# Where rows begin in SBUF: h buffers with rows 832 columns apart instead of 772, the context at column 544, and everything behind them moved by 32 bytes

## The reference

```python
for l in range(DEPTH):                                   # DEPTH = 2
    sh1, sc1, gt1, sh2, sc2, gt2 = split(silu(c) @ w_ada[l] + b_ada[l])      # and the same of c_ctx
    h  = rmsnorm(x,   g_mix[l]) * (1 + sc1)  + sh1       # latent tokens
    hc = rmsnorm(ctx, g_mix[l]) * (1 + csc1) + csh1      # context tokens
    q, k, v, u = split_in(h @ w_in[l])                   # hc goes through the same weights
    a_out  = latent_attention(rope(q), rope(k), v, k_ctx, v_ctx, attn_sink[l])
    cv_out = silu(layernorm(depthwise_conv31(glu(u))))
    x = x + gt1 * (concat(rmsnorm(a_out), rmsnorm(cv_out)) @ w_out[l])
    h2 = rmsnorm(x, g_ffn[l]) * (1 + sc2) + sh2
    x = x + gt2 * ((silu(h2 @ w_gate) * (h2 @ w_up)) @ w_down[l])             # D_FF = 2816
    # the context goes the same way in layer 0; in layer 1 only its keys and values are needed
return rmsnorm(x, g_final)
```

## The kernel before

| operand of a gemm | start before | length of a row | start after | length of a row after |
|---|---|---|---|---|
| weights, `w_high`, `w_low` | 0 | 512, so all 0 | 0 | the same |
| `h_high`, `h_low`, columns from 0 | 0, 16, 32 ... 112 for k = 0 to 7 | 3,088 | 32 for every k | 3,328 |
| the same, context | 8, 24 ... 120 | | 32 for every k | |
| `ff_high`, `ff_low`, both ranges | 32 for every k | 3,072 | 32 | 3,072 |
| `attn_high`, `attn_low`, both ranges | 0 for every k | 3,072 | 32 | 3,072 |
| `conv_high` / `conv_low` | 0 and 64 in turn / 0 | 3,264 / 3,072 | 32 and 96 / 32 | the same |
| `k_stacked`, `q_stacked`, `prob`, `v_tokens`, `probT` | 0 | multiples of 128 | 32 | the same |
| `ff_last_*`, `h_normal_*` | 0 | 2,048 | 0 | 2,048 |

## Time and profile before

### The profile page before, as it was taken

The page is one execution under the profiler, slowest core; times in us unless marked ns, Lnnn a source line. Parts: engine busy times, 40 slices in busy tenths (PEclk is TensorE's granted clock), DMA queues, the critical chain, the costliest instruction groups (busy, mean ns, idle before and its releaser), DMA issues.

```text
span 1577.4 us, 22649 instructions
## 1 busy us (share of the span) xinstructions
PE 1519.3 (96%) x8802; PEld 1229.0 (78%) x8802; DVE 919.2 (58%) x1511; ACT 537.1 (34%) x866; POOL 128.6 (8%) x163
## 2 busy tenths in 40 slices
PE   6999988999999999999999999998999999999996
PEld 3865764688888888888888888675579788888885
DVE  2584689777666425665753466677877533333335
ACT  3312368724322112221122243137835322222222
POOL 0033221040000000000000001511020000000000
PEclk9999999999999999999999999999999999999998
DMA  9582600013323124333421123510012233333222
GB/s 357 211 225 77 239 15 28 1 41 120 120 107 120 54 93 143 116 114 133 168 92 61 54 66 117 142 54 1 28 56 92 84 103 94 93 97 103 93 89 84
DMA packets 39865, 161.16 MB, mean 102 GB/s; under 512 B 5616, under 2 KB 6000, under 8 KB 33648
## 3 DMA queue, kind: packets, MB, share of 16 engines
q1 hardware_dynamic: 35856, 148.72, 27.9%
q0 software_dynamic: 3936, 11.45, 2.7%
HBM read 149.76 MB, written 2.10 MB: 96 GB/s over the span
## 4 chain that ended last, share of the span: by engine, by line
PE 86%; DVE 6%; ACT 4%; issue 2%; POOL 1%; DMA 1%; SPq 0%; DVEq 0%; ACTq 0%; POOLq 0%
PE banks L514 74%; PE banks L543 3%; PE banks L649 2%; PE banks L451 1%; PE banks L676 1%; PE banks L661 1%; DVE row_max L1195 1%; PE banks L713 1%; ACT prob L859 1%; PE banks L483 1%; PE banks L501 1%; POOL z_padded L1630 1%; DMA ada_first<-in_w_ada 1%; ACT probT L871 1%; ACT w_high L776 0%
## 5 line engine op out<-in xcount | busy, mean ns | idle before, releaser
L776 ACT ACTIVATE w_high<-raw 128x1024 fp32r<-128x1024 f32 (+1 forms) x178 | 185.2, 1041 | 719.3 <-PE banks L514 705.8
L1078 DVE TENSOR_TENSOR w_low<-raw,w_high 128x1024 fp32r<-128x1024 f32 (+1 forms) x178 | 216.5, 1216 | 233.7 <-ACT w_high L776 230.3
L514 PE MATMUL banks<-h_high,w_high 128*128 128x512 f32 (+1 forms) x1248 | 310.8, 330 | 4.6 <-DVE w_low L1078 2.4
L514 PE MATMUL banks<-h_high,w_low 128*128 128x512 f32 (+1 forms) x1248 | 304.8, 325 | 0.0
L514 PE MATMUL banks<-h_low,w_high 128*128 128x512 f32 (+1 forms) x1248 | 304.0, 325 | 0.0
L514 PEld LDWEIGHTS banks<-h_high,w_high 128*128 128x128 f32 x1248 | 193.3, 189 | 38.6 <-issue 15.2
L514 PEld LDWEIGHTS banks<-h_low,w_high 128*128 128x128 f32 x1248 | 193.5, 189 | 20.9
L514 PEld LDWEIGHTS banks<-h_high,w_low 128*128 128x128 f32 x1248 | 192.0, 189 | 20.4
L1122 DVE COPY shift_product<-banks 128x2 f32<-128x2 f32 x78 | 12.4, 159 | 208.5 <-PE banks L514 197.6
L514 PE MATMUL banks<-h_normal_high,w_high 128*128 128x512 f32 x304 | 119.1, 392 | 2.7 <-DVE h_normal_low L1469 2.7
L514 PE MATMUL banks<-h_normal_high,w_low 128*128 128x512 f32 x304 | 119.1, 392 | 0.0
(11 more groups left out here) (192 smaller groups left out, 2200.3 us busy)
## 6 DMA issues: line engine op xcount, KB each, us to landing
raw<-in_w_gu SPq DMA_DIRECT2D x88, 512.0 KB, 3.5
ada_raw<-in_w_ada SPq DMA_DIRECT2D x21, 1024.0 KB, 5.6
raw<-in_w_dn SPq DMA_DIRECT2D x32, 512.0 KB, 3.5
raw<-in_w_mix SPq DMA_DIRECT2D x28, 512.0 KB, 5.0
ada_in_ff<-in_w_ada SPq DMA_DIRECT2D x12, 1024.0 KB, 5.6
raw<-in_w_out SPq DMA_DIRECT2D x16, 512.0 KB, 3.6
ada_first<-in_w_ada SPq DMA_DIRECT2D x7, 1024.0 KB, 14.6
raw<-in_w_dn SPq DMA_DIRECT2D x16, 384.0 KB, 3.1
```

The lines of the kernel that those rows point to most:

```text
L514: last = mm(bank[:, 2 * slot + bk, 0:b - a], weights[w][:, k0_w + k, :], rhs[:, k0_rhs + k, a:b], start=(k == 0 and n == 0), stop=(k == kt ...
L776: f(wH[j][:, 0:k, :], raw[j][:, 0:k, :], ACT.Copy).then_inc(w_high, 1)
L1078: tt(wL[j][:, 0:k, :], raw[j][:, 0:k, :], f32(wH[j][:, 0:k, :]), ALU.subtract).then_inc(w_low, 1)
```

## The change

It sets the length of a row of `h_high` and `h_low` to 832 columns and the start of the context in it to column 544, puts 32 bytes ahead of `h_high`, and keeps the shift columns and the column ranges of the matmuls the same in number. The 30 columns between the latent shift columns and the context, and the 30 at the end of a row, are not used. The gap of 32 bytes ahead of `ff_high` is gone, as the buffers behind `h_low` now start 32 bytes into a line by themselves, and `ff_last_high` gets a gap of 96 bytes instead. The region for descriptors of dynamic DMAs is 8,192 bytes per partition instead of 16,384. The instructions, their number, their order and their semaphores are otherwise those of before.

```diff
-HC = N + 2
-HW = HC + L + 2
+HC = N + 32
+HW = HC + L + 32
+LINE = 8
...
+        sb("gap_line_h", [P, LINE])
         with ExitStack() as h_scope:
             hH = h_scope.enter_context(nc.sbuf_tensor("h_high", [P, DT, HW], F32R))
...
-                s.enter_context(nc.sbuf_tensor("gap_ff", [P, 2 * max(CHUNKS) * T + 16], F32))
+                s.enter_context(nc.sbuf_tensor("gap_ff", [P, 2 * max(CHUNKS) * T], F32))
...
-                s.enter_context(nc.sbuf_tensor("gap_line", [P, 8], F32))
                 aH = s.enter_context(nc.sbuf_tensor("ff_high", [P, max(CHUNKS), T], F32R))
...
+                s.enter_context(nc.sbuf_tensor("gap_line", [P, 32 - LINE], F32))
                 lastH = s.enter_context(nc.sbuf_tensor("ff_last_high", [P, max(CHUNKS), N], F32R))
...
-            return [(0, 0, N), (1, HC, HW)] if context else [(0, 0, N // 2), (1, N // 2, HC)]
+            return [(0, 0, N), (1, HC, HC + L + 2)] if context else [(0, 0, N // 2), (1, N // 2, N + 2)]
...
             def shift_high(layer, shift):
-                for at in (N, HW - 2):
+                for at in (N, HC + L):
...
             def shift_low(layer, shift):
-                for at in (N, HW - 2):
+                for at in (N, HC + L):
...
-    nc = bacc.Bacc("TRN2", target_bir_lowering=False, num_devices=1)
+    nc = bacc.Bacc("TRN2", target_bir_lowering=False, num_devices=1, dynamic_dma_scratch_size=8192)
```

## The result

The changed kernel takes 1587.23 us (median of 5 runs, 1587.02 to 1589.47), the kernel before 1579.37 us beside it on the same chip (5 runs, 1576.3 to 1581.44). The ratio is 1.0059 with a 95% interval of 1.0047 to 1.0071, so 7.4 to 11.2 us more. Predicted were 1574.7 us, 5.4 less, and a range up to 1578.5.

A forecast was written before the change was run, and what follows sets the result against it. TensorE was taken as the bound, gemm phases lasting as long as their matmuls. Terms of 4.8 + 0.6 = 5.4 us off 1579.26 gave 1573.9, or 1574.7 as the median of runs; the range was 1571.5 to 1578.5.

The forecast's parts named there:

- the h pairs: Gemms reading h, 1,440 pairs of 512 and 258 columns: from 350.8 to 347.5 ns each, 4.8 us less.
- oa of layer 1: Lone matmuls of 512 columns reading attn, moved off byte 0: taken as 0, with up to 0.3 us more.
- `ff_last` and `h_normal` stay at byte 0: Operands of lone matmuls, held not to move within a line of 128 bytes, so no change in time.
- GpSimd's wait: Rival: z copies in layer 1 wait for room in the halved scratch; about 1610 us if each waits; chance 0.04.
- The same for every k: Sign in layer 0's gu phases: h pairs step by 347.5 ns, equal for every k, as each row begins alike.
- slope of 0.415 ns per column: Cost per column from ff's pair and a lone 512, pricing the two shift columns of h at 0.8 ns.
- The halves of layer 1: 432 pairs of 256 and 258 columns at 237.9 ns: taken as 0, with 1.4 us either way.
- oa of layer 0: 96 pairs reading attn, moved from byte 0 to 32: from 353.3 to 346.7 ns, 0.6 us less.
- ob of layer 0: 96 pairs reading conv, moved to bytes 32 and 96: taken as 0, between 0.2 us less and 0.4 more.
- Attention: Scores, values and transposes in both layers, operands moved from byte 0 to 32: taken as 0, at most 3.2 us either way.
- Placement is not the cause: Rival for the gemm pairs: shift columns and buffer contents explain the differences, change worth nothing, 1580.1 us; chance 0.07.
- Only broken groups of 16 bytes: Rival for h pairs: only the context's start off a multiple of 16 costs, 2.4 us gained, 1577.7 us; chance 0.05.

The follow-up runs named there:

- e4_last_128: The kernel before with 128 bytes ahead of ff_last_high and nothing else changed: 1588.4 us, ratio 1.0061.
- e2_last_back: The changed kernel with the gap ahead of ff_last_high 128 bytes longer, so ff_last and h_normal return to byte 128 of 256: 1579.21 us, ratio 1.0003.
- m1_places: The map: only gemm matmuls, computation left out, moved rows started at places 16 bytes apart: lone 226.7 to 234.5 ns, pairs of 512 and 258 346.7 to 353.3.
- e3_lines_256: e2_last_back with h rows of 896 columns and the context at column 576, so both ranges begin at byte 160 of 256: 1575.88 us, ratio 0.9975.
- e7_all_at_128: The kernel before with h rows of 896 columns, context at 576 and half the scratch, all of h at byte 128 of 256: 1580.59 us, ratio 1.0006.
- e1_scratch_only: The kernel before with only the scratch cut to 8,192 bytes, every buffer 8,192 bytes lower: 1579.2 us, ratio 1.0002.
- e6_context_552: e2_last_back with the context at column 552 instead of 544, at byte 64 of 256 instead of 32: 1582.21 us, ratio 1.0015.
- m2_entries: Computation left out; seven placements of matmuls each timed behind five forerunners: 160 + 64 took 346.7 or 353.3 ns, the other targets one step each.

## Why the prediction was wrong, by its own steps

**What the trace says of the sum.** The prediction had 5.4 us off, the distances say 7.7 on. The 13.1 between them are 9.0 for `ff_last` and `h_normal`, 3.6 for the h pairs, 0.6 for oa of layer 1 and 0.4 for ob, less 0.5 for the halves.

**The step that failed** is "`ff_last` and `h_normal` stay at byte 0", with "ff, `ff_last` and `h_normal` do not move" drawn from it. It was true within a line of 128, the only unit that the prediction counted in; no row had been read that shows such a unit. Within 256 these operands (of `h_normal` the low part) went from the weights' own byte to 128 past it, and the step from 226.7 to 232.3 and 233.3 ns: +9.0 us where 0 stood. `e4_last_128` makes that loss alone and `e2_last_back` takes it away, so it is shown. The rows for doubting were there: the earlier trace rows mixed bytes 0 and 64 of 128, and the same nominal byte 0 gave the *slowest* pair (attn, 353.3) and the *fastest* lone matmul (226.5). One byte with both signs says that a place is not good or bad by itself, or that it isn't one byte. (Within 256 it is one, 128: the map shows that pairs and lone matmuls have their lowest steps at different places.) The rival on the slow side was GpSimd's wait; none had this mechanism, and 1,440 lone matmuls that "stay" turned out to carry more time than any edit.

**The h pairs** were to give 4.8 us and gave 1.2; the prediction's own sign of being wrong, "if h pairs stay at 350", came. The rule "same byte of a line as ff" was carried out for the long range only; the context came to 32 of 256 where ff has 160. The map has 350.0 for 160 + 32, which the changed kernel shows exactly, and `e3_lines_256` the 346.7 of ff. "The same for every k", which the prediction called more telling, did not come either: over the k of a tile in `gu1` the step goes through 349.4, 348.9, 351.1 and 350.6 ns in turn, though each k begins at the same two bytes (before, 349.8 to 353.9). In `e3_lines_256` it is 346.7 for each. Equal places for each k are no gain by themselves (`e7_all_at_128`).

**The slope of 0.415 ns per column** was wrong. It was worked out from a lone matmul at its best place and a pair at its best, two different places; two columns more cost 0.0 (346.7 for 256 and for 258). **The halves of layer 1**, taken as 0 with 3.3 ns either way, gained 1.2 ns a pair. The forecast's own range, 1571.9 to 1577.5, is 2.8 us either way, where the three terms named for it add up to 3.1; that has no part in the miss.

**oa of layer 0** was right, 346.7 ns and 0.6 us. **ob of layer 0** was within its bound (0.3 more, up to 0.4 allowed). **oa of layer 1** was taken as 0 with 0.3 us more as its bound, by the 230.0 of conv; it took 0.6, since 160 for a lone matmul is 233.3 and conv's 230.0 was a mixture that holds such steps. A mean over places was used as an end of a range.

**Attention** was right at 0: the windows 205 to 311 and 1075 to 1148 us of the changed kernel, the first answering to the earlier trace rows, and last the second in the kernel before:

```profile
205.00:311.00 106.00, 94.81 (x575) 59.59 (x575) 88.75 (x277) 86.27 (x216) 12.60 (x8) 0.98 0.04 11
1075.00:1148.00 73.00, 67.57 (x425) 43.60 (x425) 58.01 (x179) 59.19 (x142) 4.22 (x4) 0.95 0.05 15
...
1075.00:1148.00 73.00, 67.55 (x425) 43.59 (x426) 58.03 (x179) 59.11 (x142) 4.22 (x4) 0.95 0.05 15
```

The two attentions take the same time to 0.2 us: from the last h product ahead to the first product of ob, 98.1 and 98.3 us in layer 0, 77.0 and 77.1 in layer 1.

Transposes were named as the test of the stationary side. In the changed kernel (min, median, max in ns) the loads of `prob`, which moved by 32 bytes, take what those of `act_out` take, which did not:

```profile
L663 PEld LDWEIGHTS banks<-ident,prob x240: 137/141/237, 219.2 to 1142.5; 128*128 128x128 f32 x120
...
L663 PEld LDWEIGHTS banks<-ident,act_out x80: 137/140/143, 224.0 to 1144.0; 128*128 128x128 f32 x80
```

**DVE, ACT and the scratch** were right at 0: issues of 496 ns and a landing of 3.0 us at the median, 9.2 at most, above; and `e1_scratch_only`. The Trainium skill's page "DMA: Bandwidth & Descriptors", section "Terms", has 16 bytes for a descriptor; the estimate from it, by which the smaller ring would not fill, fits that.

**"Placement is not the cause"** falls: ten kernels here have the same instructions in number and kind, differ in nothing but places (and the scratch, which costs nothing), and lie between 1574.5 and 1588.4 us. The Trainium skill's page "SBUF — State Buffer", section "Who interferes with whom", gives TensorE two independent read ports and says that it never waits on anyone. In `e4_last_128` a gap of 32 columns, with the other engines' work unchanged, makes each of 1,440 matmuls some 6 ns dearer. The measurement decides: the cost of a matmul depends on where its moving operand lies relative to its weights (`m1_places`), which this rule leaves out. **"Only broken groups of 16 bytes"** falls too, since the changed kernel's context begins on a multiple of 16 for each k and steps by 350.0.

**What stays open.** By what mechanism a matmul takes 6.6 ns more when its rows begin 128 of 256 bytes further was not found; the runs show that the place relative to the weights counts, not how. Nor is it known why a pair is fastest 32 bytes to either side of the weights and a lone matmul at their own byte, why all three products of `h_normal` slow down when only its low part moves, or why 160 + 64 and 128 + 128 have two steps.

## What to carry to other kernels

When a change moves buffers, list the place of **every** operand behind it, relative to the operand that it is read with, and over more than the unit that you believe in; an operand that "stays" under one unit may move under the next. Before you rest a forecast on a unit, look for a pair of rows that would contradict it: the same place both slowest and fastest in this trace was one. And where TensorE is the bound in long runs of equal matmuls, measure a map of places by itself first: the map here had the step of every placement that was then built but one, `e6_context_552`, whose place has two steps. Totals followed less well: `e7_all_at_128` lost 0.9 us where the steps said 4.5. So before a placement is trusted, time it behind more than one forerunner, and in the kernel.

## What the runs showed of the hardware

- In float32r gemms with one weight load for each matmul, the distance from one matmul of 512 columns to the next is 226.7 ns when the moving rows begin at the weights' own byte within 256, and 231 to 234.5 at nearly all others, 128 bytes past among them (232.8); 64 past has 228.9 (`m1_places`). For pairs of 512 and 256 or 258 it is 346.7 at 32 bytes to either side, and mostly 353.3 at the weights' own byte.
- Means over 24 steps come in levels: 346.7, 350.0, 353.3 ns for most pairs, 226.7 and 233.3 for most lone matmuls. Single steps within them differ (236, 234 and 230 ns for the three products of `h_normal`). Between 256 and 258 columns there is no difference where the level is the same.
- Two placements, with the weights at 128, have two steps, 346.7 and 353.3 ns, each held for a whole block of 36 pairs: ranges at 160 and 64, where what ran before decides which, and ranges at 128 and 128, where 346.7 came once in 12 blocks (`m2_entries`).
- The granted clock fell to 0.50 for 3.4 us in the gemm phases at different places in different executions of the same work, for about 1.5 us each (966.0 us in the changed kernel, where the kernel before stayed at 1.00).
- Half the scratch for dynamic DMAs cost nothing that can be told with 3,936 packets on that queue (ratio 1.0002, 0.9991 to 1.0013), nor did a shift of all buffers by 8,192 or by 128 bytes together.
